# Half of the value table streamed for two token tiles as one-hot weight products, and one chain of side work across the row phases

## The reference, cut to what matters

```python
def body(xb):                      # 128 tokens at a time
    q = (xb @ peer_wq).reshape(PEER_TBLOCK, PEER_HEADS, 2, PEER_QDIM // 2)
    s = jnp.einsum('thpd,phkd->thpk', q, peer_subkeys)
    # two top-16 per head, 16 x 16 sums, top-16 of these: 16 experts of 16384 for each of 8 heads,
    # with softmax weights g; then, for each token, over its 8 * 16 = 128 experts e:
    # a[e] = gelu(h . peer_u[e]) * g[e];   y = sum of a[e] * peer_v[e]
```

## Time and profile before

| | us |
|---|---|
| median of 3 runs | 2530.08 |
| the profiled execution, its time | 2523.41 |
| its span | 2521.5 |
| DVE busy | 1757.8 (70%) |
| PE busy | 1236.1 (49%) |
| POOL busy | 1159.6 (46%) |
| bytes read from HBM | 937.36 MB |

### The profile page before, as it was taken

The page is one execution under the profiler, slowest core; times in us unless marked ns, Lnnn a source line. Parts: engine busy times, 40 slices in busy tenths (PEclk is TensorE's granted clock), DMA queues, the critical chain, the costliest instruction groups (busy, mean ns, idle before and its releaser), DMA issues.

```text
span 2521.5 us, 17792 instructions
## 1 busy us (share of the span) xinstructions
PE 1236.1 (49%) x6337; PEld 668.1 (26%) x6337; DVE 1757.8 (70%) x2243; ACT 213.1 (8%) x559; POOL 1159.6 (46%) x686
## 2 busy tenths in 40 slices
PE   6799989892943541456857961000025556100000
PEld 3444434740422321343324930000012222000000
DVE  1011021158779976996559568999999997899898
ACT  3110032000010320220001010000000000000000
POOL 1000000012446643763124306688876666787784
PEclk9899989896975555657985975555558776655555
DMA  9979999659999989999998989999999999999897
GB/s 318 381 316 422 398 357 267 236 196 405 400 401 375 410 345 350 412 411 348 322 416 311 423 304 422 361 404 422 422 414 420 414 411 413 420 422 422 367 422 303
DMA packets 150658, 944.49 MB, mean 375 GB/s; under 512 B 18155, under 2 KB 32051, under 8 KB 44446
## 3 DMA queue, kind: packets, MB, share of 16 engines
q0 software_dynamic: 94784, 682.66, 67.3%
q1 hardware_dynamic: 55791, 260.74, 28.3%
HBM read 937.36 MB, written 10.26 MB: 376 GB/s over the span
## 4 chain that ended last, share of the span: by engine, by line
DMA 28%; PE 24%; DVE 22%; POOL 16%; issue 9%; SPq 1%; ACT 1%; POOLq 0%; DVEq 0%; ACTq 0%
POOL arena L666 11%; DMA arena<-in_peer_u,arena 11%; DMA arena<-in_peer_v,arena 8%; DVE arena L1974 7%; DMA arena<-in_w_out 5%; DVE arena L1997 5%; POOL arena L678 4%; DMA arena<-in_w_ada 4%; PE PS L1444 3%; PE PS L1467 3%; PE PS L1165 2%; PE PS L1252 2%; PE PS L964 2%; PE PS L1073 2%; DVE arena L2027 2%
## 5 line engine op out<-in xcount | busy, mean ns | idle before, releaser
L666 POOL DMA_INDIRECT arena<-in_peer_u,arena x256 | 458.8, 1792 | 457.2 <-DVE arena L1974 256.3
L1974 DVE CUSTOM_DVE_ANT_0 arena<-arena 128x2048 f32<-128x2048 f32 x256 | 581.3, 2288 | 119.3 <-DMA arena<-in_peer_u,arena 118.0
L1997 DVE SCALAR_TENSOR_TENSOR arena<-arena 128x2048 f32<-128x2048 f32 x226 | 531.1, 2350 | 133.7 <-DMA arena<-in_peer_v,arena 128.2
L666 POOL DMA_INDIRECT arena<-in_peer_v,arena x256 | 416.6, 1627 | 380.1 <-DVE arena L1997 243.9
L1467 PE MATMUL PS<-arena 128*128 128x512 f32 x240 | 173.3, 889 | 453.1 <-DMA arena<-in_peer_v,arena 448.3
L1467 PEld LDWEIGHTS PS<-arena 128*128 128x128 f32 x240 | 66.6, 291 | 560.3 <-issue 554.6
L1473 PE MATMUL PS<-arena 128*64 128x512 f32 x8 | 5.3, 824 | 346.1 <-DVEq L2040 346.1
L2030 DVE SCALAR_TENSOR_TENSOR arena<-arena 128x2048 f32<-128x2048 f32 x64 | 150.6, 2353 | 11.0 <-DMA arena<-in_peer_v,arena 5.3
L2027 DVE CUSTOM_DVE_ANT_0 arena<-arena 128x2048 f32<-128x2048 f32 x64 | 144.8, 2291 | 8.2 <-DMA arena<-in_peer_u,arena 6.5
L964 PE MATMUL PS<-arena 128*32 128x512 f32 x768 | 118.0, 714 | 66.1 <-DMA arena<-in_w_ada 62.9
L678 POOL DMA_INDIRECT arena<-in_peer_v,arena x64 | 126.6, 1978 | 39.0 <-issue 18.6
(11 more groups left out here) (341 smaller groups left out, 1824.3 us busy)
## 6 DMA issues: line engine op xcount, KB each, us to landing
arena<-in_w_ada SPq DMA_DIRECT2D x96, 1024.0 KB, 12.9
arena<-in_w_in SPq DMA_DIRECT2D x32, 1048.0 KB, 10.3
arena<-in_peer_wq SPq DMA_DIRECT2D x32, 1024.0 KB, 10.4
arena<-in_w_in SPq DMA_DIRECT2D x32, 768.0 KB, 9.6
arena<-in_w_out SPq DMA_DIRECT2D x16, 1024.0 KB, 33.7
arena<-in_w_out SPq DMA_DIRECT2D x32, 512.0 KB, 26.8
arena<-in_peer_u,arena POOLq DMA_INDIRECT x320, 12.8
arena<-in_peer_v,arena POOLq DMA_INDIRECT x320, 13.1
```

What stands on the lines that cost most here:

```text
L666: pool.indirect_dma_start(out=rows_ring[:, k % NROW, :], out_offset=None, in_=tables[kind], in_offset=bass.IndirectOffsetOnAxis(ap=ids[:, ...
L1974: V.tensor_tensor_reduce(out=buf, in0=buf, in1=h2(t), scale=1.0, scalar=0.0, op0=ALU.mult, op1=ALU.add, accum_out=dots[:, t, r:r + 1]).the ...
L1997: V.scalar_tensor_tensor(out=acc[t], in0=rows_ring[:, k % NROW, :], scalar=dots[:, t, r:r + 1], in1=acc[t], op0=ALU.mult, op1=ALU.add).the ...
```

## The change

**Half rows.** In v0 and v1 a row fetches only columns 0 to 1023 of `peer_v` (0.5 MiB for 128 partitions), and the DVE sum is 128x1024. `peer_v` is viewed as twice as many rows of half the width, and `eid2` holds the doubled ids. Twelve half cells (eight in v1) take the place of the six buffers.

**The other half as a product.** For tiles 0 and 1 the columns 1024 to 2047 come from a dense product: `WT[t]` (128 x 16384 for 128 tokens) holds the weight of each expert for each token, and `peer_v[:, 1024:2048]` is streamed whole by SP in 128 blocks of 128 rows (0.5 MiB each, four buffers `vd`), each used by four PE products of 128x512 for the two tiles. `WT` is built by four tokens at a time: DVE and ACT make one-hot matrices of the two id digits (one of them weighted), PE multiplies them (128 columns a token), and ACT copies the result out. That is 32 groups for each tile. Those of tile 0 run in u1, those of tile 1 in the first 32 rows of v1. The stream waits for all 64 groups (`s_wmm`), but for its first two blocks.

**One chain.** The four generators become one, `chain`, which goes on over the borders of the phases; `reach` makes DVE run it up to a named step before the rows that need it. Most pauses are gone, attention works two units ahead, and top-k is done in parts of 2, 2 and 4 heads (`PARTS`), so that the first rows need two heads of tile 0. ACT does `expert_exp(0, 1)` and `(0, 2)` behind its copies of z.

**The rest.** Tile 2 has no loops any more, PE no rows of v1; x1 of tiles 1 and 2 is parked in HBM and read back; the ends of tiles 0 and 1 come after the last row of tile 2. SBUF regions are laid out anew.

```diff
+GC = 1024
+DC = D - GC
+N_BLK = 128
+N_VD = 4
+N_GRP = 32
+HOT_ACT = (4, 2)
+OUT_PAUSE, WQ_PAUSE = (20, 28), 60
+PARTS = [[(0, 2), (2, 2), (4, 4)], [(0, 2), (2, 2), (4, 4)], [(0, 4), (4, 4)]]
...
@@ SP
+            for i in range(N_BLK):
+                if i == 1:
+                    sp.wait_ge(s_dots, 2)
+                if i == 2:
+                    sp.wait_ge(s_wmm, 2 * N_GRP)
+                wait(sp, s_vused, i - N_VD + 1)
+                sp.dma_start(vd[i % N_VD], I["peer_v"][rows_of(i), GC:D]).then_inc(s_vin[i % N_VD], 16)
@@ POOL
+            half_rows = I["peer_v"].rearrange("n (a d) -> (n a) d", a=D // GC)
+            for kind, t in PHASES:
                 for r in range(NROWS[t]):
...
+                    wait(pool, s_rowfree, row_former[k] + 1)
+                    pool.indirect_dma_start(out=row_buffer(kind, t, k), out_offset=None, in_=table, ...)
@@ ACT
-            expert_exp(0)
+            expert_exp(0, 0)
...
+            expert_exp(0, 1)
+            expert_exp(0, 2)
             A(GK[:, 1, :], PS[:, 2, 0:48], exp, scale=-1.0).then_inc(s_gexp, 1)
...
+            def one_hot(t, g):
+                n = N_GRP * t + g
+                wait(act, s_wmm, n - 1)
+                for j in range(HOT_ACT[t]):
+                    token = 4 * g + j
+                    last = A(hot2[:, g % 2, j, :], iota128, ACT.Abs, bias=i2N[:, token:token + 1], scale=1.0)
+                last.then_inc(s_abs, 1)
+                act.wait_ge(s_abs, n + 1)
+                v = hot2[:, g % 2, 0:HOT_ACT[t], :]
+                A(v, v, ACT.Relu, bias=ones_col, scale=-1.0).then_inc(s_hot2, 1)
...
+                    act.wait_ge(s_wmm, N_GRP * t + g + 1)
+                    A(WT[t][:, :, 4 * g:4 * g + 4], PS[:, 4 + g % 2, :].rearrange("p (t i) -> p i t", t=4), copy).then_inc(s_wev, 1)
@@ PE
+            pe.wait_ge(s_wev, 2 * N_GRP)
+            for i in range(N_BLK):
+                pe.wait_ge(s_vin[i % N_VD], VIN_BASE[i % N_VD] + 16 * (i // N_VD + 1))
+                for t in range(2):
+                    for n in range(2):
+                        last = mm(PS[:, 2 * t + n, :], WT[t][:, i, :], vd[i % N_VD][:, n * SECTION:(n + 1) * SECTION], start=(i == 0), stop=(i == N_BLK - 1))
+                last.then_inc(s_vused, 1)
@@ DVE
-                yield from pause(Q_PAUSE)
-                yield from pause(K_PAUSE)
+                yield from experts(0, 2)
...
+                for u in range(8, 16):
+                    p_norm(u)
+                    yield
+                    if u + 2 < 16:
+                        p_max(u + 2)
+                        yield
...
                 for b in range(DB):
+                    smp_norm(b)
                     yield from pause(2)
-                    smp_norm(b)
...
+                    if b + 2 < DB:
+                        s_max(b + 2)
+                        yield
...
                 yield from pause(WQ_PAUSE)
-                yield from experts(1, 0)
+                for part in range(3):
+                    yield from experts(1, part)
+                yield
                 shares(1)
+                for part in range(2):
+                    yield from experts(2, part)
...
+                ids(0)
+                yield from pause(2)
+                yield from one_hots(0)
...
+            def one_hots(t):
+                for g in range(N_GRP):
...
+                    for j in range(HOT_ACT[t], 4):
+                        V.tensor_scalar(hot2[:, g % 2, j, :], iota128, i2T[:, token:token + 1], None, ALU.is_equal)
+                    for j in range(4):
+                        last = V.tensor_scalar(hot1[:, g % 2, j, :], iota128, i1T[:, token:token + 1], wT[:, token:token + 1], ALU.is_equal, ALU.mult)
+                    last.then_inc(s_hot1, 1)
+                    yield
...
+            dot_rows(1, beside)
+            for _ in beside:
+                pass
+            weights(1, acc[1])
+            ids(1)
+            beside = one_hots(1)
+            sum_rows(1, acc[1], beside)
```

More of the change, by code:

```diff
@@ new lines, in _ @@
+            beside = chain()
+            dot_rows(0, beside)
+            shares(0)
+            weights(0, acc0)
+            sum_rows(0, acc0, beside)
+            link(V.tensor_copy(acc[0], acc0))
+            dot_rows(1, beside)
[5 more added lines that the diff above has]
+            sum_rows(1, acc[1], beside)
+            for _ in beside:
+                pass
+            dot_rows(2, iter(()))
@@ new lines, in _ @@
+            weights(2, acc[2])
+            sum_rows(2, acc[2], iter(()))
+            dve.sem_inc(s_facc, 1)
+            for t in range(2):
+                finish(t)
+            dve.wait_ge(s_fold, N_RS + 1)
+            dve.wait_ge(s_gs2, N_RT + 4)
+            for i in range(4):
+                cols = slice(i * SECTION, (i + 1) * SECTION)
+                last = V.tensor_tensor(acc[2][0:TS, cols], PS[0:TS, i, :], GBs[0:TS, cols], ALU.mult)
+            link(last)
+            V.tensor_tensor(acc[2][0:TS, :], acc[2][0:TS, :], XB[2][0:TS, :], ALU.add).then_inc(s_y, 1)
```

484 lines of the change are left out of this document (249 added, 235 removed).

## The result

The changed kernel takes 2565.03 us in the median of four runs (2557.64 to 2566.42), the kernel before, run beside it, 2530.67 (2529.5 to 2531.51): a ratio of 1.0138 (95% interval 1.0118 to 1.0158), so 34 us **slower**. I had forecast 2475 and faster, with a range up to 2560. The profiled execution took 2566.4 us, its span is 2564.5.

A forecast was written before the change was run, and what follows sets the result against it. DMA was taken to bound u1 to v2, a PE chain the end of v0. First row of u1 at 1348, u1 388 us, stream from 1832, 615 us to 2447, tail 20: span 2467, median 2475 us; range 2415 to 2560.

The forecast's parts named there:

- Bytes: Whole kernel: half rows save 134 MB, stream adds 67, parking x1 adds 4; 63 MB less, 152 us at 414 GB/s.
- Rate of 4 KB pieces: Half rows and stream: DMA in 4 KB pieces runs at 414 GB/s, with 281 as the other end of the bound.
- Rival 6: Half rows and stream: 4 KB pieces are slow, 230 us more (2705) or 160 more (2635); chance 0.02.
- u0 and the first row of u1: Start through v0: the steps of the chain summed, putting the first row of u1 at 1348 instead of 1505.
- The first row of u1 as the pivot: Start of u1: must come before about 1402 or the kernel is slower; with u1 at 1450 it takes 2577.
- rival 2: Start of u1: u1 comes late, after about 1402, and the kernel is slower; chance 0.07.
- u1: Phase u1: 286 us for 87 rows with the chain, 102 for 41 DMA-paced rows; 388 us, 42 longer than before.
- Weights in v1: First 32 rows of v1, with six one-hots each: 2.6 us a row, 83 us; bounds 42 to 160.
- Clock and rest: Stream to end: PE at 2.4 GHz, 255 MB in 615 us until 2447, then a tail of 20 us.
- Rival 3: Stream: PE at the lower clock, 0.889 us an instruction, 128 blocks take 910 us; median 2770; chance 0.05.
- Rival 1: All phases: DMA alone decides, chain and DVE hide behind transfers; 2364, or about 2420; chance 0.14.
- Rival 4: u1 and v1: building weights costs 5 us a group, 77 us more in v1, about 60 in u1; 2610; chance 0.04.

The follow-up runs named there:

- a4: Changed kernel with one row more between steps of attention units and samples, and longer pauses beside w_out (34 and 36 rows): 2527.18 us, ratio 1.000.
- c3: Kernel of b1 plus early bias of the compressed scores, with attention chunks of w_out loaded from 128 contiguous (wrong) rows: 2488.36 us, 28 less than its base.
- b1: Kernel of a4 with tile 0's gelu moved between the copies of gate 1 and pauses beside w_out of 21 and 26 rows: 2522.81 us.
- b4: Changed kernel with the pause before the second residual add cut from 28 to 18 rows: 2575.46 us, ratio 1.0205.
- a1: Changed kernel with only 2 of 32 groups of weights built for each of tiles 0 and 1, stream kept whole: 2495.64 us.
- c1: Kernel of b1 plus early bias, without tile 2's top-k (copies of tile 1's experts and weights instead): 2472.11 us, 45 to 47 less than its base.
- d3: Kernel before the change with only the new layout of attention outputs and contiguous chunks of w_out: 2495.07 us, ratio 0.9875.
- c4: Kernel of b1 plus early bias, with ACT making three instead of two unweighted one-hots of a group for tile 1: 2506.58 us.

## Why the prediction was wrong

The number that failed is the date of the first row of u1, 1450 for 1348. But what the runs show behind it is not a late date: it is that DVE has no slack from the scores of tile 1 to the end of the building, and that steps hold rows before that.

- **Bytes** (63 MB, 152 us): right, 61 MB and 148 us.
- **Rate of 4 KB pieces** (414): right for half rows and stream, 405 to 417. Rival 6 fell. Its form with three quarters of 414 went by the rule of the Trainium skill, "DMA: Bandwidth & Descriptors", section "Bandwidth", of at least 1 MiB a DMA for 75% of peak; the stream's DMAs of 0.5 MiB, several in flight, ran at 413 GB/s, so the trace does not agree here. My own reason against the rule was a misreading: the pooling chunks beside which I had read 419 GB/s are DMAs of 1024 KB in pieces of 4 KB, and the attention chunks are those of 512 KB.
- **u0 and the first row of u1** (1348): wrong, 1450, the step that failed. It went wrong in pieces:

| us | forecast | measured |
|---|---|---|
| first row of u0 | 541 | 546 |
| normed k | 712 | 738 |
| first attention unit | 746 | 788 |
| end of the samples | 914 | 999 |
| `w_out` on PE, its length | 148 | 169 |
| first row of v0 | 1067 | 1146 |
| scores of tile 1 ready | 1245 | 1335 |
| first row of u1 | 1348 | 1450 |

The normed k is a step of DVE behind rows. I took a row beside `w_in` at 3.6 us; from 592 to 684 DMA was full and a row took 4.6, so DVE had done 36 rows at 702 and not 43, and PE waited:

```profile
PE PS L1209 <- DVEq L1998: 52.9, 1, 52.9
```

The bias of the compressed scores (13.5 us, SP's order behind `w_pool`) I had not read. For an attention unit I summed the work of PE and DVE (8 us) and let rows run beside it. The unit took 10 with two rows in it, and the samples 127 us instead of 88: a step that waits holds the rows. This overlap was wrong as a mechanism, and a4 prices the held rows, 38 us. `w_out` I sized by the rate of the earlier trace rows. I took that rate as given, where c3 shows it to go with the 64 partitions, and still had 21 us too few. From the scores to u1 I had 103 us and it took 115.
- **The first row of u1 as the pivot** (break-even 1402, "with u1 at 1450 it takes 2577"): near as a sum, 2565 came, so rival 2 is what happened, at 0.07 far too low. But that is partly luck, for as a mechanism it is wrong. b1 and b4 made the scores 23 and 25 us earlier and gave nothing at the start of v1; a4 had u1 at 1368 and gave 38 us, not 82, since it had left two parts of the top-k for u1. Only c3, which made chain and rows earlier together, was paid nearly in full (28 us for 29). From the scores of tile 1 on DVE is the bound, and its work moves from v0 to u1 or back.
- **u1** (388): right, 392, and in its parts: the chain ended beside row 89 after 290 us, forecast row 87 and 286. **Weights in v1** (83 us for 32 rows, stream 96 us behind v1's start): 88 for the rows, 91 for the stream. What I missed is what these nearly right numbers mean: 43 and 64 us of DMA time more than before, which nothing later gives back, since DVE has no slack there. a1 prices the building at 69 us, c1 the top-k of tile 2 at 45 to 47.
- **Clock and rest** (level 2.4 GHz, 615 us from the stream's start to the last row, tail 20): right, 1.00, 612, 19. Rival 3 fell.
- Rival 1, DMA alone decides, fell hardest: the account has 294 us of DMA time lost, 195 more than before. Rival 4 fell too: 2.77 us a group, not 5.
- **Slips that did not decide.** By the earlier trace rows DVE is busy 74 to 94% of a phase, not from 64. PE was busy 98 and 94% of the two stretches of the earlier trace rows that I gave for the clock. The 0.889 us of the earlier trace rows are the mean duration of one product, while 0.447 is busy time for each; busy time for each was 0.72 in v1 before. 128 one-hots at 0.2 us are 26 us, not 28, and one took 0.28. In rival 2 the two workings differ: 42 + 83 + 5 - 7 is 123, which puts the break-even at 1382; the other gives 1402.

## What to carry to other kernels

Write the account of the bound resource before the forecast: for each phase what it moves, what it loses, and which engine is full while it loses. A change that takes bytes out of one phase and puts DVE work into the next two saves nothing if DVE is full there; then the unit to count in is DVE microseconds. The date of a first row is a measure only if as much work is left behind it as before. Ask of a stretch with full DMA whether its rate is full too. And where side work is cut into steps between rows, a step that waits costs its wait in rows: give it rows enough to wait beside.

## What the hardware showed that was not expected

- Beside DMAs of 64 partitions everything is slower, at a full share: 327 for 411 GB/s over 50 us, and 182 for 146 ns a packet in the rows' own queue. Contiguous rows over 128 partitions gave back 28 us in c3 and 33 in d3.
- DMAs to 128 partitions whose source has 2 as its outermost dimension ran at 52 GB/s (share 0.13): same bytes, and the kernel took 167 us more than b1.
- PE slowed to one instruction in 2.1 to 2.8 us for some 60 us in five kernels, and not in c3, c4 or d3 with the same 512 products of `peer_wq`. In the profile this is "issue", not a wait, and its cause is open.
- DVE's one-hot of 128x128 takes 0.28 us in a run of four (1.12 us), and a group of six beside a half row runs with no gap, 2.77 us.
